# Exchanging a rotation's halves by DMA, two tiles in turns behind a norm, and a group norm by groups, in a fused two-block kernel

## The reference, cut to what matters

```python
def rms_norm(x, g):          # ahead of every FFN, the mixing and each layer
    y = x * lax.rsqrt(jnp.mean(x * x, axis=-1, keepdims=True) + EPS)
    return y * g

# end of the mixing sublayer: y is 512 x 768, 4 groups of 192
y = rms_norm(y.reshape(b, L, 4, 192), ssd_norm.reshape(4, 192)).reshape(b, L, 768)
out = jnp.concatenate([fourier_mix(u_f, fourier_w), y], axis=-1) @ w_out

def rope(x, pos):            # on qB, kB, qI, kI, qC, kC, qD, kD of each layer, heads of 64
    x1, x2 = x[..., :32], x[..., 32:]
    return jnp.concatenate([x1 * cos - x2 * sin, x2 * cos + x1 * sin], axis=-1)

# a layer's FFN
u = causal_dwconv(h @ w_up, conv_w, conv_b); a, b = jnp.split(u, 2, axis=-1)
x = x + (silu(a) * b) @ w_down
```

## Time and profile before

| | |
|---|---|
| time, median of 3 runs | 3737.37 us (3733.82 to 3743.4) |
| the profiled execution | 3741.84 us, span 3740.5 us |
| TensorE matmul (PE) | 3531.7 us busy, 94%, 17424 instructions |
| TensorE weight load (PEld) | 2777.5 us, 74% |
| VectorE (DVE) | 1702.6 us, 46%, 3129 instructions |
| ScalarE (ACT) | 1440.1 us, 38%, 2446 instructions |
| GpSimd (POOL) | 1418.1 us, 38%, 651 instructions |
| granted TensorE clock, mean | 0.97 |

### The profile page before, as it was taken

One profiled execution on the slowest core, in us unless ns is written; L12 is line 12 of the kernel. 1 busy time (PEld: TensorE's weight loads), 2 busy tenths in 40 slices (PEclk: granted clock), 3 DMA queues, 4 the chain that ended last, 5 costly groups with the idle time before them and its releaser, 6 DMA issues.

```text
span 3740.5 us, 45132 instructions
## 1 busy us (share of the span) xinstructions
PE 3531.7 (94%) x17424; PEld 2777.5 (74%) x17424; DVE 1702.6 (46%) x3129; ACT 1440.1 (38%) x2446; POOL 1418.1 (38%) x651
## 2 busy tenths in 40 slices
PE   6999999998799999999999999999989999999998
PEld 4788889785578877767666778887856766678886
DVE  7876553556410126845542233134755553234143
ACT  3223354554432223344443334342334443334342
POOL 3454433321244444324332444444423332344443
PEclk9999999999999998999999999998999999999999
DMA  7574345221123322212122222323212222223332
...
DMA packets 109974, 364.90 MB, mean 98 GB/s; under 512 B 12608, under 2 KB 13504, under 8 KB 109504
## 3 DMA queue, kind: packets, MB, share of 16 engines
...
...
## 4 chain that ended last, share of the span: by engine, by line
PE 77%; DVE 13%; ACT 5%; issue 2%; DMA 1%; POOL 1%; SPq 0%; DVEq 0%; POOLq 0%; ACTq 0%
PE ps L1308 24%; PE ps L1310 22%; PE ps L1309 22%; PE ps L1552 1%; ACT b L1636 1%; PE ps L1573 1%; DVE b L2174 1%; DVE b L2467 1%; PE ps L1534 1%; DVE b L2466 1%; DVE b L2210 1%; DVE b L2155 1%; POOL b L2538 1%; DVE b L2440 1%; PE ps L1530 1%
## 5 line engine op out<-in xcount | busy, mean ns | idle before, releaser
L2538 POOL TENSOR_TENSOR b<-b,b 128x1024 fp32r<-128x1024 f32 (+2 forms) x579 | 1324.3, 2287 | 2042.0 <-ACT b L1636 2037.0
L1308 PE MATMUL ps<-b,b 128*128 128x512 f32 (+3 forms) x4848 | 1866.2, 385 | 80.1 <-POOL b L2538 23.3
L1309 PE MATMUL ps<-b,b 128*128 128x512 f32 (+3 forms) x4848 | 1804.9, 372 | 0.0
L1310 PE MATMUL ps<-b,b 128*128 128x512 f32 (+3 forms) x4848 | 1804.5, 372 | 0.0
L1308 PEld LDWEIGHTS ps<-b,b 128*128 128x128 f32 x4848 | 934.4, 193 | 348.0 <-issue 139.3
L1310 PEld LDWEIGHTS ps<-b,b 128*128 128x128 f32 x4848 | 934.3, 193 | 161.5
L1309 PEld LDWEIGHTS ps<-b,b 128*128 128x128 f32 x4848 | 936.1, 193 | 145.8 <-issue 4.8
L1636 ACT ACTIVATE b<-b 128x1024 fp32r<-128x1024 f32 (+2 forms) x622 | 607.3, 978 | 261.9 <-PE ps L1310 239.0
L2078 DVE SCALAR_TENSOR_TENSOR b<-ps,b,b 128x511 f32<-128x511 f32 x88 | 66.0, 750 | 371.0 <-ACT b L1687 371.0
L2174 DVE CUSTOM_DVE_ANT_0 b<-b,b,b 128x1024 bf16<-128x1024 f32 x112 | 210.0, 1875 | 20.1 <-DMA b<-in_ada 8.4
L1697 ACT ACTIVATE b<-b 128x512 fp32r<-128x512 f32 (+1 forms) x110 | 64.9, 590 | 390.2 <-DVE b L2087 287.8
...
## 6 DMA issues: line engine op xcount, KB each, us to landing
...
```

Of the source, the lines that this page charges most:

```text
L1308: pe.matmul(out, a[0], b[0], start=first, stop=False)
L1309: pe.matmul(out, a[0], b[1], start=False, stop=False)
L1310: return pe.matmul(out, a[1], b[0], start=False, stop=last)
L2538: then(pool.tensor_tensor(wlo[j % NS][:, 0:nk * w], raw[j % NR][:, 0:nk * w], whi[j % NS][:, 0:nk * w].bitcast(F32), ALU.subtract), "lop", j)
```

## The change

Three things are changed.

1. **The rotation.** The sign of the sine table is turned round. ScalarE copies the bank into `Q` as before, and then issues four DMAs from its own queue that copy `Q`'s 32-partition pieces crosswise into the destination (64 KB each), signalling `d_half0` or `d_half1`; the waits for a free destination move there. In ScalarE's queue the DMAs stand between the evacuation and the next split of weights. The bank is free after the copy. VectorE has one product of 128 x 512 in place (part 0) and the sum (part 1), both with inputs in SBUF alone; both engines' products, GpSimd's cosine one too, wait for the DMAs. Part 0 now stands five k rows behind the evacuation, part 1 two further.
2. **Two tiles in turns.** `both` takes two chunks at once and lets their tiles' k rows alternate. It is used for the first gate and up tile of each FFN (`jj == 0`: five FFNs) and for the two `qi` tiles of each layer. The next chunk's `begin` step, which splits weights, stands behind the pair.
3. **The grouped norm by groups.** `gn2` and `gn3` are done per group; group 0 of a half needs its first two tiles, group 1 the second and third. Group 0 scales and passes on tile 0, group 1 the other two. So the first half's steps stand one pair earlier in part, and in the second half group 0 is done ahead of `yv` of the last pair. k row 5 of the first three `w_out` tiles moves into the woven part, whose rate goes from 1.4 to 1.1.

The numbering (`number`) and the semaphores follow. The diff, without context lines (`@@` gives the line in the kernel before, then the new one):

```diff
@@ -173 +173 @@
-    c["cos"], c["sin"] = np.cos(ang), np.where(pi < 32, 1.0, -1.0) * np.sin(ang)
+    c["cos"], c["sin"] = np.cos(ang), np.where(pi < 32, -1.0, 1.0) * np.sin(ang)
@@ -244,0 +245,14 @@
+    def both(self, key, *tiles):
+        c = [self.begin(key), self.at[0]]
+        assert self.stream[c[1]][0] == key and self.stream[c[0]][3] == self.stream[c[1]][3] == 8
+        self.at[0] += 1
+        for k in range(8):
+            for t, ch in zip(tiles, c):
+                self.step("mm", t=t, c=ch, q=k, k=k, first=k == 0, last=k == 7, done=k == 7)
+                self.spent(3 * t["N"] / 2400.0)
+        self.step("begin", c=c[1])
+        for t, ch in zip(tiles, c):
+            t["c"] = ch
+        return tiles
@@ -274 +288 @@
-            self.tail = [dict(kind="rope", t=t, part=p) for p in range(5)]
+            self.tail = [None] * 5 + [dict(kind="rope", t=t, part=0), None, dict(kind="rope", t=t, part=1)]
...
@@ -329,0 +346,4 @@
+                if jj == 0:
+                    for t in F.both(key, *[dict(name=x, i=0, N=N, ver=ver, f=f, conv=conv) for x in ("fg", "fu")]):
+                        F.step("evac", t=t)
+                    continue
@@ -404,3 +424,6 @@
-    def groupnorm(hf):
-        return ([do("gn1", hf=hf, o=o) for o in range(3)] + [do("gn2", hf=hf), do("gn3", hf=hf)]
-                + [do("gn4", hf=hf, o=o) for o in range(3)] + [do("gn5", hf=hf, o=o) for o in range(3)])
+    def groupnorm(hf, o):
+        own = (0, 1) if o == 0 else (2,)
+        done = (0,) if o == 0 else (1, 2)
+        return ([do("gn1", hf=hf, o=x) for x in own] + [do("gn2", hf=hf, o=o), do("gn3", hf=hf, o=o)]
+                + [do("gn4", hf=hf, o=x) for x in done] + [do("gn5", hf=hf, o=x) for x in done])
@@ -426,2 +449,3 @@
-            first = groupnorm(0)
-            B += [do("yv", k=k - 1)] + {3: first[:5], 4: first[5:]}.get(k, [])
+            B += [do("yv", k=k - 1)] + (groupnorm(0, k - 2) if k in (2, 3) else [])
+            if k == 5:
+                B += groupnorm(1, 0)[:2]
@@ -441 +465,3 @@
-    S += weave(F, [do("yv", k=5)] + groupnorm(1), 1.4)
+    for t in tiles:
+        part(F, t, range(5, 6))
+    S += weave(F, groupnorm(1, 0)[2:] + [do("yv", k=5)] + groupnorm(1, 1), 1.1)
@@ -446 +472 @@
-        part(F, t, range(5, 8))
+        part(F, t, range(6, 8))
@@ -490 +516,4 @@
-        F.rope("qi", 2, "qi", ver=H, l=l)
+        pair = F.both("qi", *[dict(name="qi", i=m, N=L, ver=H, l=l) for m in range(2)])
+        for t in pair:
+            F.step("evac", t=t)
+        F.tail = [None] * 4 + [dict(kind="rope", t=t, part=p) for t in pair for p in range(2)]
@@ -636,2 +665 @@
-            if name not in ROPES:
-                held[t["bank"]] = False
+            held[t["bank"]] = False
@@ -679,0 +708 @@
+                t["freed"] = ("ra", name, l, i)
@@ -681,2 +709,0 @@
-                mark("rp", name, l, i)
-                t["freed"] = ("rv", name, l, i)
@@ -708,2 +735,2 @@
-            if s["part"] == 3:
-                held[t["bank"]] = False
+            if s["part"] == 0:
+                mark("rp", t["name"], t["l"], t["i"])
...
@@ -1502,7 +1526,6 @@
-                hf = st["hf"]
-                at.wait_ge(*n("gs", hf, 2))
-                for o in range(2):
-                    b = bank_of(st["bank"][o])
-                    pe.matmul(b[:, :], ones, gsq[2 * o], start=True, stop=False)
-                    pe.matmul(b[:, :], split2[:, o, :], gsq[1], start=False, stop=True).then_inc(up("gp", hf, o), 1)
-                    freed[st["bank"][o]] = ("gl", hf, o)
+                hf, o = st["hf"], st["o"]
+                at.wait_ge(*n("gs", hf, 1 + o))
+                b = bank_of(st["bank"])
+                pe.matmul(b[:, :], ones, gsq[2 * o], start=True, stop=False)
+                pe.matmul(b[:, :], split2[:, o, :], gsq[1], start=False, stop=True).then_inc(up("gp", hf, o), 1)
+                freed[st["bank"]] = ("gl", hf, o)
@@ -1733,0 +1757,9 @@
+                    if name == "qb":
+                        at.wait_ge(*n("sqp", l, 3, 3))
+                    elif name in ("qd", "kc"):
+                        at.wait_ge(*n("s1", "A", l, 31))
+                    elif name == "qc":
+                        at.wait_ge(*n("s1", "B", l, 31))
+                    at.wait_ge(*n("ra", name, l, i))
+                    for o in range(0, 128, 32):
+                        act.dma_start(ropes[name][o:o + 32, i, :], Q[x % 2][o ^ 32:(o ^ 32) + 32, :]).then_inc(s[f"d_half{x % 2}"], 16)
...
@@ -1895,7 +1927,5 @@
-                at.wait_ge(*n("gp", hf, 1))
-                for o in range(2):
-                    act.activation(gsq[2 * o], PB[st["bank"][o]][:, :], ACT.Ln, bias=eps[:, :], scale=1.0 / 192).then_inc(
-                        up("gl", hf, o), 1)
-                at.wait_ge(*n("gl", hf, 1))
-                for o in range(2):
-                    act.activation(gsq[2 * o], gsq[2 * o], ACT.Exp, scale=-0.5).then_inc(up("ge", hf, o), 1)
+                at.wait_ge(*n("gp", hf, o))
+                act.activation(gsq[2 * o], PB[st["bank"]][:, :], ACT.Ln, bias=eps[:, :], scale=1.0 / 192).then_inc(
+                    up("gl", hf, o), 1)
+                at.wait_ge(*n("gl", hf, o))
+                act.activation(gsq[2 * o], gsq[2 * o], ACT.Exp, scale=-0.5).then_inc(up("ge", hf, o), 1)
...
@@ -2143,2 +2173,2 @@
-                b, dst = PB[t["bank"]], ropes[name]
-                if part == 0:
+                dst, x = ropes[name], rope_order.index((name, l, i))
+                if st["part"] == 0:
@@ -2146,12 +2176,2 @@
-                    at.wait_ge(*n("ra", name, l, i))
-                    if name == "qb":
-                        at.wait_ge(*n("sqp", l, 3, 3))
-                    elif name in ("qd", "kc"):
-                        at.wait_ge(*n("s1", "A", l, 31))
-                    elif name == "qc":
-                        at.wait_ge(*n("s1", "B", l, 31))
-                if part < 4:
-                    o, f = 32 * part, 32 * (part ^ 1)
-                    p = dve.tensor_tensor(dst[o:o + 32, i, :], b[f:f + 32, :], sin[f:f + 32, :], ALU.mult)
-                    if part == 3:
-                        p.then_inc(up("rv", name, l, i), 1)
+                    at.wait_ge(s[f"d_half{x % 2}"], 64 * (x // 2 + 1))
+                    dve.tensor_tensor(dst[:, i, :], dst[:, i, :], sin, ALU.mult).then_inc(up("rv", name, l, i), 1)
@@ -2161,2 +2181 @@
-                    q = Q[rope_order.index((name, l, i)) % 2]
-                    dve.tensor_tensor(dst[:, i, :], dst[:, i, :], q[:, :], ALU.add).then_inc(up("rope", name, l, i), 1)
+                    dve.tensor_tensor(dst[:, i, :], dst[:, i, :], Q[x % 2][:, :], ALU.add).then_inc(up("rope", name, l, i), 1)
@@ -2361 +2380 @@
-                at.wait_ge(*n("ge", hf, 1))
+                at.wait_ge(*n("ge", hf, min(o, 1)))
@@ -2557 +2576 @@
-            elif k == "evac":
+            elif k == "rope" and st["part"] == 0:
@@ -2559,7 +2578,6 @@
-                name, i, l = t["name"], t["i"], t.get("l")
-                if name in ROPES:
-                    q = Q[rope_order.index((name, l, i)) % 2]
-                    behind()
-                    at.wait_ge(s["d_cs"], 16 * (l + 1))
-                    at.wait_ge(*n("ra", name, l, i))
-                    then(pool.tensor_tensor(q[:, :], q[:, :], cos, ALU.mult), "rp", name, l, i)
+                name, i, l = t["name"], t["i"], t["l"]
+                x = rope_order.index((name, l, i))
+                behind()
+                at.wait_ge(s["d_cs"], 16 * (l + 1))
+                at.wait_ge(s[f"d_half{x % 2}"], 64 * (x // 2 + 1))
+                then(pool.tensor_tensor(Q[x % 2][:, :], Q[x % 2][:, :], cos, ALU.mult), "rp", name, l, i)
```

25 lines of the change are left out of this document (12 added, 13 removed).

## The result

The changed kernel takes 3814.31 us in the median (3812.16 to 3817.7) against 3738.69 us for the kernel before, timed beside it: a ratio of 1.0201, 95% interval 1.0189 to 1.0214. It is 75.6 us slower, where 28 us faster was forecast. Its profiled execution has a span of 3810.9 us.

The account below looks back on a forecast made before the run. TensorE's waits and lower clock were taken to bound the kernel. Gains of 13 (pairs) and 16 (rotation) less 1 (group norm) made 28 us: 3741.84 to 3713.8 profiled, 3709 us in the median, range 3692 to 3732.

Parts of the forecast that it names:

- What bounds the kernel: Whole kernel: TensorE carries 77% of the chain of waits; time only where it stands still or runs at the lower clock.
- Part 1: Two tiles in turns behind a norm, seven places: products follow without a hole, 13 us gained.
- the six starts: Norm-fed tile pairs: a sign of being right, third tile starting 13 to 13.5 us after the first product.
- Part 2: The rotation, 44 tiles: 26.5 - 13 + 5 - 2 = 16 us gained, bounds 6 lost and 36 gained.
- two tiles of cover: ScalarE's queue: four transfers, 1.8 us per tile, stand ahead of the next weight split, which has this cover.
- the hold of VectorE: Each rotation: product and cosine product released by the same landing, with the sum about 2.7 us, against 3.5 before.
- the 8 tiles that were worked out in detail: The two `qb` stages: 26.5 us of waits can go, 13 us of new ones come, 5 us from the clock.
- Part 3: Group norm by groups, end of the scan: TensorE resumes near 971; 1 us lost, bounds 6 lost and 6 gained.
- I take nothing: Group norm's first half: two chains of some 6 us enter VectorE's and ScalarE's queues, with TensorE work ready; no effect counted.
- (b): Rotation: landing late, VectorE's queue stands ahead of softmax rows; 43 us lost against 28 gained, 3752 us; chance 0.07.
- Rival (a): Rotation gives nothing, still costing TensorE 3.3 us each through the held queue; the pairs stay; 3725 us; chance 0.12.
- signs of being wrong: VectorE idle over 2 us per tile; `qd`, `kc`, `qc` waits over 10 us; group norm resumption over 5 us later.

Follow-up runs that it names:

- the pairs: Two tiles in turns alone, with old rotation and old group norm, on the kernel before: 3730.0 us, ratio 0.997.
- the rotation issued by SP: The rotation by DMA alone on the kernel before, its four DMAs issued from SP's queue in place of ScalarE's: 3734.85 us, ratio 0.9983.
- the rotation alone: The rotation by DMA applied to the kernel before, without the other two parts: 3815.48 us, ratio 1.0197.
- the cosine first: The rotation by DMA without the other parts, GpSimd's cosine product put ahead of the next weights' low part: 3817.12 us, ratio 1.0205.
- The second half: Group norm by groups on the kernel before, only the second half's steps in the new order: 3745.23 us, ratio 1.0012.
- the first half: Group norm by groups on the kernel before, only the first half's steps in the new order: 3751.47 us, ratio 1.0032.
- the sum later: The rotation by DMA without the other parts, the sum moved to two k rows behind the next evacuation: 3797.66 us, ratio 1.0148.

## Why the prediction was wrong, point by point

**What bounds the kernel** was read rightly: TensorE, its waits and its clock. Two of the three places aimed at gain when their part is done well: the pairs 0.3%, the rotation issued by SP 0.17%. No run of the group norm's new order gained anything.

**Part 1, 13 us gained (bounds wide): right.** 11 us were measured (0.3%, 0.19 to 0.4%). Over the six starts the third tile begins 12.6 to 13.8 us after the first product, where 13 to 13.5 was said. In the two `qi` pairs, 13.7 us each, TensorE waited for GpSimd's low part just ahead of the third tile, 1.26 and 0.63 us. At layer 0's FFN it is 13.5 us:

```profile
2239.79 0.77 PE L1332 MATMUL ps<-b,b 128*128 128x512 f32 x1 [3.71 <-DVE b L2073]
...
2253.29 0.39 PE L1332 MATMUL ps<-b,b 128*128 128x512 f32 x1
```

**Part 2, 16 us gained (bounds 6 lost, 36 gained): wrong, 74 lost.** The step that failed is the one costed at nothing: ScalarE's issues stand "ahead of the next weight split, which has two tiles of cover". The cover was there for TensorE: it waits 24.0 us for GpSimd's low part with the rotation alone, against 23.3 us before. But the split also times the low part, and that now fell on the landing. The same four issues behind the split, or in SP's queue, take the loss away (3740.65 and 3734.85 us). A step moved under cover is free only for those who wait for its result, not for those who share its queue.

With that term went the hold of VectorE, "about 1.30 + 0.69 + 0.69 = 2.7 us". It has no low part in it, and was 4.6 us. The sentence on GpSimd, "its cosine product (1.30 us) now waits for the landing too, with the next weights' low part behind it in its queue", also had the order the wrong way round. Part 0 of the rotation stands five k rows behind the evacuation, the `begin` that splits the next weights right behind it; so the low part comes first. The order of GpSimd's queue could be listed before the run, and I looked at VectorE's alone. But the misread order is not what cost the time: in the kernel with the cosine first, the order that the prediction assumed, VectorE was held 4.7 us and the time was 3817.12 us.

The second failure is a sum: "the `qd`, `kc`, `qc` tiles lie where TensorE hardly waits; their saving is hidden, and ScalarE's 1.8 us and the held sums cost 2 us in all (bounds 0 and 20)". TensorE waited 61.6 us there, in place of 5.8. A stage without waits has only so much slack. A ring that grows by more leaves a wait at every tile, 2.56 us in the one read above. The four issues were 2.44 us, not 1.8; the landing 2.0 us and not 2.5: both of the right size. In these stages the granted clock was 0.95 and 0.93, where it had been 1.00.

In the `qb` stages the old 3.0 us wait for the bank did go, and in layer 0 the waits for the scaled rows fell from 10.3 to 3.9 us (window 1573 to 1640), but 6.0 us of waits for ScalarE came in, which no term had. So in the 8 tiles that were worked out in detail the sign was right and the saving smaller. VectorE lost 15 us of busy time in the changed kernel (29 with the rotation alone), where over 30 was said, since its product was stretched (2.26 us in the mean).

**Part 3, 1 us lost (bounds 6 and 6): wrong, 15 lost.** The second half, for which the working was done, lost 5 us (0.02 to 0.21%), within its bounds of 6. With it alone TensorE resumes at 975.26, not near 971 as worked out (967.72 before):

```profile
962.68 0.75 DVE L2367 SCALAR_TENSOR_TENSOR b<-b,b,b 128x512 f32<-128x512 f32 x1 [9.06 <-ACT b L1905]
...
975.26 0.80 PE L1315 MATMUL ps<-b,b 128*128 128x512 f32 x1 [4.37 <-DVE b L2374]
```

VectorE waited 9.06 us for the first group's exponential, where about 7 was taken for all of that group's steps.

The term that failed is "I take nothing" for the first half: 12 us (0.18 to 0.45%). It named the mechanism, two chains of some 6 us in VectorE's and ScalarE's queues, and set against it the work ready for TensorE; that was less than the chains.

**The rivals.** The one on the slower side, (b), had the place right, VectorE's queue standing in front of the softmax rows, and the sign; its cause, a late landing, was not there. Its price, 43 us beyond the forecast, was less than half of the 90 us by which the rotation missed it (74 lost, 16 gained forecast). Rival (a) assumed a hold that stays as it is, and not a longer one. The Trainium skill's rule on the shared ports ("SBUF — State Buffer", section "SBUF: two separate sides"), which its lock rows show too, is seen in the changed kernel, where the product takes 2.7 us at the median beside the low part. In the tile read above that decided nothing; with the cosine first and with the sum later it did lengthen the chain.

**The signs.** Two of the three signs of being wrong came: new waits of more than 10 us in the `qd`, `kc`, `qc` stages, and the late resumption behind the last group norm. The third, over 2 us of idle per tile ahead of the product, did not: 66.7 us over 44 tiles is 1.5 us each.
